# Seven products of halves in place of eight in nine of eleven steps of each up map

## The reference

```
h = rmsnorm(x, norm_ffn[i])                 # 512 x 1024
up = einsum("bsd,df->bsf", h, w_up)         # 1024 -> 2 * 2816
act, gate = up[..., :2816], up[..., 2816:]
act = causal_dwconv(act, w_dw, b_dw)        # width 3 over positions
x = x + einsum("bsf,fd->bsd", silu(act) * gate, w_down)
```

## Time and profile before

| what | us |
|---|---|
| median of 3 runs | 938.58 |
| lowest and highest of them | 938.08, 939.66 |
| span of the profiled execution, first to last instruction | 937.5 |
| PE busy in it | 926.4 |
| PE weight loads (PEld) busy | 778.3 |
| DVE busy | 542.8 |
| ACT busy | 365.8 |
| POOL busy | 87.0 |

### The profile page before, as it was taken

One profiled execution on the slowest core, in us unless ns is written; L12 is line 12 of the kernel. 1 busy time (PEld: TensorE's weight loads), 2 busy tenths in 40 slices (PEclk: granted clock), 3 DMA queues, 4 the chain that ended last, 5 costly groups with the idle time before them and its releaser, 6 DMA issues.

```text
span 937.5 us, 12821 instructions
## 1 busy us (share of the span) xinstructions
PE 926.4 (99%) x5028; PEld 778.3 (83%) x5028; DVE 542.8 (58%) x689; ACT 365.8 (39%) x479; POOL 87.0 (9%) x78
## 2 busy tenths in 40 slices
PE   8999999999999999999999999999999999999997
PEld 7888888888888888888888898888888888888887
DVE  6999986576555556654343468755555555532333
ACT  7653566443333333332222454533333333322331
POOL 0575824000000000000000020000000000000000
PEclk9999999999999999999999999999999999999999
DMA  7323030222233222221323331322222232223212
GB/s 256 118 90 113 12 106 28 108 90 91 89 100 118 95 89 89 95 88 62 121 68 118 110 135 51 130 89 89 89 89 89 95 116 74 80 83 114 92 62 90
DMA packets 18558, 89.66 MB, mean 96 GB/s; under 512 B 2528, under 2 KB 5856, under 8 KB 11488
## 3 DMA queue, kind: packets, MB, share of 16 engines
q1 hardware_dynamic: 17952, 88.72, 27.8%
q10 hardware_dynamic: 576, 0.52, 0.2%
HBM read 86.09 MB, written 2.10 MB: 94 GB/s over the span
## 4 chain that ended last, share of the span: by engine, by line
PE 95%; DVE 2%; POOL 1%; issue 1%; SPq 0%; DMA 0%; ACT 0%; DVEq 0%; POOLq 0%
PE bank L1127 28%; PE bank L1128 28%; PE bank L1129 28%; PE bank L1169 1%; PE bank L1204 1%; PE bank L1187 1%; DVE sumsq L1091 1%; DVE h_lo L1057 1%; SPq L306 0%; PE bank L1193 0%; PE bank L1221 0%; PE bank L1461 0%; PE bank L1493 0%; PE bank L1465 0%; PE bank L1466 0%
## 5 line engine op out<-in xcount | busy, mean ns | idle before, releaser
L1127 PE MATMUL bank<-h_hi,w_hi 128*128 128x512 f32 x784 | 306.1, 390 | 0.0
L1129 PE MATMUL bank<-h_hi,w_lo 128*128 128x512 f32 x784 | 305.0, 389 | 0.0
L1128 PE MATMUL bank<-h_lo,w_hi 128*128 128x512 f32 x784 | 305.0, 389 | 0.0
L493 ACT ACTIVATE w_hi<-w_raw 128x2048 fp32r<-128x2048 f32 (+2 forms) x87 | 147.3, 1693 | 232.0 <-PE bank L1129 231.1
L796 DVE TENSOR_TENSOR w_lo<-w_raw,w_hi 128x2048 fp32r<-128x2048 f32 (+2 forms) x81 | 162.1, 2002 | 100.8 <-ACT w_hi L493 100.0
L1127 PEld LDWEIGHTS bank<-h_hi,w_hi 128*128 128x128 f32 x784 | 147.2, 188 | 31.3 <-issue 0.5
L1129 PEld LDWEIGHTS bank<-h_hi,w_lo 128*128 128x128 f32 x784 | 147.1, 188 | 30.8
L1128 PEld LDWEIGHTS bank<-h_lo,w_hi 128*128 128x128 f32 x784 | 147.2, 188 | 30.6 <-issue 0.5
L1128 PE MATMUL bank<-u_lo,w_hi 128*128 128x512 f32 (+1 forms) x406 | 153.3, 378 | 0.0
L1127 PE MATMUL bank<-u_hi,w_hi 128*128 128x512 f32 (+1 forms) x374 | 141.0, 377 | 0.0
L1129 PE MATMUL bank<-u_hi,w_lo 128*128 128x512 f32 (+1 forms) x374 | 140.8, 377 | 0.0
(11 more groups left out here) (208 smaller groups left out, 914.8 us busy)
## 6 DMA issues: line engine op xcount, KB each, us to landing
w_raw<-w_up SPq DMA_DIRECT2D x44, 1024.0 KB, 4.8
w_raw<-w_down SPq DMA_DIRECT2D x32, 704.0 KB, 4.0
w_raw<-w_pw SPq DMA_DIRECT2D x11, 1024.0 KB, 5.2
x_res<-x SPq DMA_DIRECT2D x3, 512.0 KB, 7.3
out<-out_sb SPq DMA_DIRECT2D x12, 128.0 KB, 1.8
w_raw<-w_pw SPq DMA_DIRECT2D x4, 256.0 KB, 6.9
gathered<-stage SPq DMA_DIRECT2D x32, 32.0 KB, 2.3
w_raw<-w_pool SPq DMA_DIRECT2D x2, 512.0 KB, 3.7
```

The costliest lines, as they stand in the source:

```text
L493: nc.scalar.activation(w_hi[s][:, 0:columns], w_raw[s][:, 0:columns], ACT.Copy).then_inc(w_rounded[s], 1)
L1127: M.matmul(dst, a, hi, start=start, stop=False)
L1128: M.matmul(dst, a, lo, start=False, stop=False)
L1129: return M.matmul(dst, b, hi, start=False, stop=stop)
```

## The change

In steps 2 to 10 of both layers the product of the weights with h goes by Strassen's form in a variant with shared sums. The weights of a tile pair and h are cut in halves along the channels (2 x 4 chunks), the two tiles of act or gate are the other cut of the weights, and the positions are cut in 2 x 256. Seven products of halves take the place of eight. Numbers 1 to 7 name the products and u is 0 for act and 1 for gate: a step is 14 jobs `(product, u)` in the order `ORDER`. A job is 4 chunks x 3 passes, 12 matmuls of 256 columns, so a step is 168 of them.

h has to be whole for this: `scale_h` makes the normalised h on DVE (eight operations of 128x512), and seven sides (four of them sums or differences) are made, rounded and split once a layer (`add_sides`, `add_fourth_side`, `third_side`, `round_side`, `split_side`, 128x1024 each). The weights of a job are a block of 128x512 elements or a sum of blocks. Four of the seven operands are sums made by DVE (`first_sum`, `next_sum`, `third_sum`, `fourth_sum`). ACT rounds the 14 blocks of a step (`round_op`), POOL splits ten (`BY_POOL`) and DVE four. They go through a ring of seven slots that takes the place of `w_hi` and `w_lo`.

Products 1, 6, 7 and 4 of one u pile up in one bank, and after each of the first three ACT copies the sum so far to SBUF (`copy_first`, `copy_second`, `copy_third`). DVE adds the copies to the other bank (`add_corner`, `add_edge`). Steps use banks 0 to 3 and 4 to 7 in turn. From step 5 on, the rounding of u waits (`round_late`, `split_late`) until the sides are free, at the end of the up map.

Steps 0 and 1 stay plain, but POOL now splits `w_lo[1]` of step 1. The loops of the up map are written out. Cut to its core:

```diff
+PLAIN = (2, 2)
+FAST = [UP_STEPS - n for n in PLAIN]
+UNIT_HALF = UNIT // 2
+KH = KD // 2
...
+ORDER = [(1, 0), (1, 1), (5, 0), (5, 1), (6, 0), (6, 1), (2, 0), (7, 0), (7, 1), (2, 1), (4, 0), (3, 0), (4, 1), (3, 1)]
+PRODUCTS = len(ORDER)
+PLACE = {job: n for n, job in enumerate(ORDER)}
+RING = 7
+
+SIDES = [1, 5, 6, 2, 7, 3, 4]
+SIDE = {product: n for n, product in enumerate(SIDES)}
+
+BY_POOL = [n for n, (product, _) in enumerate(ORDER) if product in (1, 5, 6, 2, 4)]
+BY_DVE = [n for n in range(PRODUCTS) if n not in BY_POOL]
...
+        def slot_free(queue, layer, i, n):
+
+            done = job(layer, i, n) - RING + 1
+            if done > FAST_BEFORE[layer] * PRODUCTS:
+                queue.wait_ge(product_done, done)
+            elif n < 4:
+                queue.wait_ge(unit_done[0], M_UP[layer] + PLAIN[layer])
+            else:
+                queue.wait_ge(unit_done[1], M_UP[layer] + PLAIN[layer])
...
+            def split_op(layer, i, n):
+
+                product, u = ORDER[n]
+                slot = job(layer, i, n) % RING
+                pool.wait_ge(op_rounded, job(layer, i, n) + 1)
+                if product == 5:
+                    pool.wait_ge(sum2, turn(step_of(layer, i) + 1, u))
+                source = {1: raw_block(u, 0, 0), 2: raw_block(u, 1, 0), 4: raw_block(u, 1, 1), 5: ring_sum[slot][:, :, :], 6: second_sum[u][:, :, :]}[product]
+                if product == 6:
+                    pool.wait_ge(sum2, turn(step_of(layer, i) + 1, u))
+                nc.gpsimd.tensor_tensor(ring_lo[slot][:, :, :], source, as_f32(ring_hi[slot][:, :, :]), SUB).then_inc(op_by_pool, 1)
+
...
+            def fast_steps(layer):
+
+                third_side(layer)
+                split_side(layer, 1, (side1,))
+                for i in range(PLAIN[layer], UP_STEPS):
+                    for n in BY_POOL:
+                        split_op(layer, i, n)
+                        if i == PLAIN[layer] and n == 3:
+                            split_side(layer, 2, (side4,))
+                        if i == PLAIN[layer] and n == 4:
+                            split_side(layer, 7, ())
+                        if i == PLAIN[layer] and n == 5:
+                            split_side(layer, 3, (side2, side3))
+                for c in range(LATE):
+                    split_late(layer, c)
+
...
+            def plain_step(layer, i):
...
-                    nc.scalar.activation(y[:, t, :], y[:, t, :], ACT.Silu).then_inc(silu_done[t], 1)
+                    silu(layer, i, t)
+                if i == PLAIN[layer] - 1:
+                    for n in range(3, 7):
+                        round_side(layer, n)
+                        round_op(layer, PLAIN[layer], n - 3)
+                    round_op(layer, PLAIN[layer], 4)
                 for t in range(2):
 
                     act.wait_ge(drained[2 + t], f + i + 1)
-                    nc.scalar.activation(chunk(u_hi, 2 * i + t), y[:, t, :], ACT.Copy).then_inc(u_rounded[t], 1)
-                round_unit(1, m + i + 1, columns)
+                    round_u(i, t)
+                if i < PLAIN[layer] - 1:
+                    round_unit(1, m + i + 1, UNIT)
...
+                    for n in range(PRODUCTS):
+                        if n < 2 and i > first:
+                            silu(layer, i - 1, 1 - n)
+                        if n in (1, 2):
+                            copy_first(layer, i, n - 1)
+                        if n in (5, 6):
+                            copy_second(layer, i, n - 5)
+                        if n in (8, 9):
+                            copy_third(layer, i, n - 8)
+                        if n == 11:
+                            copy_low(layer, i)
+                        build(i, n + 5)
+                        if n == 11:
+                            act.wait_ge(low_copied, step_of(layer, i) + 1)
+                            act.wait_ge(corner_added, turn(step_of(layer, i) + 1, 0))
+                            conv_middle(layer, i, 1)
...
+                for c in range(8, 10):
+                    round_late(layer, c)
+                silu(layer, last, 1)
+                silu(layer, last, 0)
+                act.wait_ge(product_done, job(layer, last, PRODUCTS - 1) + 1)
+                round_unit(1, M_DOWN[layer], DOWN_UNIT)
+                for c in range(10, LATE):
+                    round_late(layer, c)
...
+            def plain_step(layer, i):
...
-                for t in range(2):
-                    dve.wait_ge(silu_done[t], n + i + 1)
+                    dve.wait_ge(silu_done[t], UP_STEPS * layer + i + 1)
                     V.tensor_tensor(y[:, t, :], y[:, t, :], rms[:, :], MUL).then_inc(act_scaled[t], 1)
+                if i == PLAIN[layer] - 2:
+                    scale_h(layer)
+                if i == PLAIN[layer] - 1:
+                    for u in range(2):
+                        first_sum(layer, PLAIN[layer], u)
+                    split_side(layer, 6, (side4,))
+                    split_side(layer, 4, ())
+                    for u in range(2):
+                        next_sum(layer, PLAIN[layer], u)
                 for t in range(2):
                     dve.wait_ge(act_scaled[t], n + i + 1)
                     dve.wait_ge(unit_done[1], m + i + 1)
                     V.tensor_tensor(y[:, t, :], bank[2 + t][:, :], y[:, t, :], MUL).then_inc(drained[2 + t], 1)
                 for t in range(2):
-                    dve.wait_ge(u_rounded[t], n + i + 1)
-                    V.tensor_tensor(chunk(u_lo, 2 * i + t), y[:, t, :], as_f32(chunk(u_hi, 2 * i + t)), SUB).then_inc(u_split[t], 1)
-                split_unit(1, m + i + 1, columns)
+                    split_u(layer, i, t)
...
+            def scale_h(layer):
...
+                norm = "ffn0" if layer == 0 else "ffn1"
+                for c in range(KD):
+                    at = (c % KH) * HT
+                    dst = (near_half if c < KH else far_half)[:, :, at:at + HT]
+                    V.scalar_tensor_tensor(dst, x_res[:, c, :].rearrange("p (h t) -> p h t", h=2), col(norm, c), rms[:, :].rearrange("p (h t) -> p h t", h=2), MUL, MUL).then_inc(h_scaled, 1)
...
+                            if i == last:
+                                split_unit(0, M_DOWN[layer], DOWN_UNIT)
+                            conv_rest(layer, i, 1)
+                            add_edge(layer, i, 0)
+                conv_rest(layer, last, 0)
+                add_edge(layer, last, 1)
+                use_gate(layer, last, 1)
+                use_gate(layer, last, 0)
+                split_unit(1, M_DOWN[layer], DOWN_UNIT)
 
...
+            def product(layer, i, n):
+
+                which, u = ORDER[n]
+                step, slot, side = step_of(layer, i), job(layer, i, n) % RING, SIDE[which]
+                if i == PLAIN[layer]:
+                    wait_side(layer, which)
+                if which in (1, 5):
+                    if i < PLAIN[layer] + 2:
+                        wait_drained(range(4), DRAINED_UP[layer] + PLAIN[layer])
+                    elif which == 5:
+                        pe.wait_ge(edge_added, turn(step - 1, u))
+                    elif u == 0:
+                        pe.wait_ge(low_copied, step - 1)
+                    else:
+                        pe.wait_ge(gate_used[1], step - 1)
+                if which == 6:
+                    pe.wait_ge(first_copied, turn(step + 1, u))
...
+                if which in (1, 6, 7, 4):
+                    dst = low_bank(i, u)[:, 0:HT]
+                else:
+                    dst = edge_bank(i, u)[:, 0:HT] if which == 2 else edge_bank(i, u)[:, HT:T]
+                for k in range(KH):
+                    a, b, hi, lo = ring_hi[slot][:, k, :], ring_lo[slot][:, k, :], side_hi[side][:, k, :], side_lo[side][:, k, :]
+                    M.matmul(dst, a, hi, start=which in (1, 5) and k == 0, stop=False, skip_group_check=True)
+                    M.matmul(dst, a, lo, start=False, stop=False, skip_group_check=True)
+                    last = M.matmul(dst, b, hi, start=False, stop=which in (2, 3, 4) and k == KH - 1, skip_group_check=True)
+                last.then_inc(product_done, 1)
```

More of the change, by code:

```diff
@@ L475, in _ @@
                 nc.gpsimd.tensor_tensor(v_lo[:, c, :], conv_out[:, c, :], as_f32(v_hi[:, c, :]), SUB).then_inc(v_split, 1)
+            for i in range(1, PLAIN[0]):
+                split(1, M_UP[0] + i)
+            fast_steps(0)
             pool.wait_ge(w_rounded[0], M_UP[1] + 1)
@@ L1498, in _ @@
                         last.then_inc(window_mm, 1)
-                up_step(layer, 0, first=True)
-                with pe.Fori(1, UP_STEPS) as i:
-                    up_step(layer, i)
+                for i in range(PLAIN[layer]):
+                    plain_step(layer, i)
+                for i in range(PLAIN[layer], UP_STEPS):
+                    for n in range(PRODUCTS):
+                        product(layer, i, n)
                 if layer == 0:
@@ L1508, in _ @@
```

(3 more changed lines are left out.)

402 lines of the change are left out of this document (343 added, 59 removed).

## The result

The changed kernel takes **1050.66 us** (median of 4 runs, 1048.88 to 1051.22) against 938.53 for the kernel before, a ratio of 1.1189 (95% interval 1.1173 to 1.1205). It is 112 us slower where I forecast no change (938.8, range 930 to 948). The profiled execution has a span of 1049.4 us.

A forecast was written before the change was run, and what follows sets the result against it. PE was taken to bound the kernel: -28.8 us of matmuls, +22.4 head, +4.1 tail and +2.5 clock sum to +0.2, so 938.8 us against 938.58, range 930 to 948.

The forecast's parts named there:

- The bound now: Whole old kernel: PE is busy 99% of 937.5 us, so only fewer or shorter matmuls win time.
- The pace of 120 ns and -28.8 us: Fast steps: 168 matmuls at 120 ns take 20.16 us, not 21.76; eighteen steps save 28.8 us.
- Each is below 20.16, so PE sets the pace: Inside fast steps: POOL 13.0, ACT 16 and DVE 16.4 us each fit in 20.16, so steady steps add 0.
- upper bound of 0.5 us a step for the chain: Steady fast steps: PE's wait for ACT's copy before job 7 taken as 0, at most 0.5 us a step (9 us).
- The head, `w_lo[1]`: Ahead of unit 1 of step 1: PE waits for POOL's late split, 4.6 us in layer 0, 6.7 in layer 1.
- The head, the first fast job: Start of the first fast job: PE waits for DVE's last gate product of step 1, 2.9 us a layer.
- POOL's queue: Head of each fast stretch: POOL delivers operands 5 and 6 late, PE waits 0.6 and 2.0 us a layer.
- The tail: Last fast step: the two first down units come 0.7 and 1.3 us late, 4.1 us in all (0 to 10).
- The clock: After PE's pauses: half pace for some 5 us costs 2.5 us, counted once; bounds 0 and 10.
- my fourth rival: Heads: the clock falls at four pauses, 7.5 us over the sum, 946.3 us; chance 0.10.
- number 3: Steady steps: the chain copy, add, tap, silu, gate falls behind 0.5 us in each of 18, +9 us, 948; chance 0.18.

The follow-up runs named there:

- the run with nothing to read in the heads: Changed kernel with GpSimd's ten splits per fast step, and its splits and side difference in the heads, replaced by memsets, those parts left out of the result: 939.85 us.

## Why the prediction was wrong, point by point

**The bound now**: right. PE set the time before.

**The pace of 120 ns and -28.8 us**: right. With the port free a step takes the 20.16 us of the forecast.

**"Each is below 20.16, so PE sets the pace"**: this step failed, and it is worth 92 of the 112 us. The load of POOL (13.0) and of DVE (16.4) was added up from durations measured apart. In the earlier trace rows DVE's 0.69 are rows without POOL beside them, and where DVE and POOL did work at the same time in the old kernel, DVE read PSUM. I set the two lists side by side where they have to be added: DVE's operations with two SBUF inputs are about 13.8 of its 16.4 us, 13.0 of POOL make 26.8. Neighbours overlap in the records, by 0.08 us on DVE and 0.04 on POOL (rows 297.85 and 297.30 above), which takes about 2 us off: some 24.8, an estimate, for the 25.8 measured in an early step, and in the same way 23.4 for the 24.6 of a late one. DVE is busy 35.87 of the 40 us from 280 to 320. My upper bound of 0.5 us a step for the chain was ten times too small. The place was the right one (`copy_first(1)` behind the last gate product), the cause was not the order but the durations along it.

**The head, `w_lo[1]`**: 4.6 + 6.7 = 11.3 forecast, 11.5 measured. Right as a wait, wrong as a cost: without it PE waits as much longer at the first fast job. Two waits in a row that end at the same chain are not a sum.

**The head, the first fast job**: 2.9 a layer forecast, 9.2 and 8.5 measured. The mis-sized term is the three operations on sides in step 0 (5.58, 3.29 and 3.42), 12.3 us where 1.22 each make 3.7, by the port. With the port free the wait is 4.8 and 3.2, so the rest of this sum was short by 1.9 and 0.3.

**POOL's queue**: 5.2 forecast, 7.0 measured, right in kind.

**The tail**: 4.1 forecast, 9.4 measured (7.7 with the port free, for the most part at the second down unit, where I had 1.3 and 3.3 came).

**The clock**: 2.5 forecast for one pause, 10 as the bound for four. It fell far oftener than that (mean 0.959), and in the fast steps it cost nothing, since PE wasn't what set them. Where PE does set the pace it costs more than I had, some 7 us in the run with nothing to read in the heads, between the 2.5 of the sum and the 10 of my fourth rival. The rule I weighed (TensorE: Matmul & The Clock Gate, "HAM oscillation", in the Trainium skill) is borne out by the trace in that half pace follows pauses such as that of 4.75 us ahead of unit 1, though not all of them.

**The rivals**: number 3 had the right wait at the right place with the wrong price (9 us for 92). The range failed because no case held that an operation of the old kernel could take more than twice as long in the new one (1.62 us for 0.69).

## What to carry to other kernels

Before work is moved to GpSimd, list what VectorE does at the same time: where both have two SBUF inputs, add their times, don't take the larger one. A duration holds only with the neighbours it was measured with, so look for a row with the same inputs and the same engine beside it. And where the work fills a chain, more of it on the one engine (all splits on VectorE, 50 us faster) can beat the shared load. Neither form beat the kernel before.
